# First value weights in idle token and probability buffers, one modulation sum a step and two behind the heads' norm, staging slots refilled later

## What is computed

```
for i in (0, 1):
    ml = silu(c) @ mod_w[i] + mod_b[i]              # 12 column blocks of 512: sh1 sc1 g1 sh2 sc2 g2
    hl = xl * (1 + sc1) + sh1                       # the context: the same with silu(c_ctx)
    i == 0: q, k, v = heads(hl @ wqkv); rope; p = softmax(q k) twice a head
            a = p[0] - lam * p[1];  o = a @ v;  o = o * rsqrt(mean(o^2) + eps) * subln
            yl = o @ wo
    i == 1: yl = pool_mixer(hl)
    xl = layer_norm(ALPHA * xl + (1 + g1) * yl)
    xl = layer_norm(ALPHA * xl + (1 + g2) * experts(xl * (1 + sc2) + sh2))
```

## Time and profile before

| | |
|---|---|
| median of 3 runs | 1258.74 us (1258.15 to 1260.99) |
| the profiled execution | 1261.48 us, of which 1259.6 us are the span from the first to the last instruction |
| busy over the span | TensorE 91%, VectorE 28%, ScalarE 13%, DMA mean 381 GB/s |
| first scores, last scores of the attention | 118.33 us, 253.18 us |
| first expert matmul of layer 0 | 325.45 us |
| granted TensorE clock, mean | 0.972 |

### The profile page before, as it was taken

One profiled execution on the slowest core, in us unless ns is written; L12 is line 12 of the kernel. 1 busy time (PEld: TensorE's weight loads), 2 busy tenths in 40 slices (PEclk: granted clock), 3 DMA queues, 4 the chain that ended last, 5 costly groups with the idle time before them and its releaser, 6 DMA issues.

```text
span 1259.6 us, 12321 instructions
## 1 busy us (share of the span) xinstructions
PE 1141.3 (91%) x5288; PEld 509.4 (40%) x5288; DVE 357.7 (28%) x729; ACT 165.1 (13%) x398; POOL 16.0 (1%) x28
## 2 busy tenths in 40 slices
PE   8969978678899999999999989899999999999995
PEld 3534544444534333343333335634333333433331
DVE  1567889734211111111111113311111111111113
ACT  1101212333200000010000002400000000100000
POOL 0000000000000000000000001000000000000000
PEclk9989988789999999999999999999999999999999
DMA  9898775955599999999999999799999999999993
GB/s 396 336 337 340 281 297 209 422 203 200 213 429 427 427 428 427 428 428 426 429 426 428 428 420 427 311 428 429 426 429 427 428 427 427 429 427 429 427 427 164
DMA packets 37129, 480.17 MB, mean 381 GB/s; under 512 B 4688, under 2 KB 5968, under 8 KB 8016
## 3 DMA queue, kind: packets, MB, share of 16 engines
q1 hardware_dynamic: 33136, 434.96, 82.0%
q0 software_dynamic: 2880, 41.94, 8.8%
q10 hardware_dynamic: 1056, 2.43, 0.6%
HBM read 476.18 MB, written 1.05 MB: 379 GB/s over the span
## 4 chain that ended last, share of the span: by engine, by line
PE 72%; DVE 12%; DMA 11%; issue 2%; ACT 2%; ACTq 0%; DVEq 0%
PE ps L849 51%; DMA ring<-in_mod_w 5%; PE ps L841 5%; PE ps L857 5%; DMA ring<-in_moe_wd 3%; PE ps L710 2%; DVE ring L1258 2%; DVE work L1572 2%; PE ps L613 2%; DVE work L1576 1%; DMA ring<-ring 1%; PE ps L865 1%; DVE modp L1258 1%; PE ps L554 1%; DMA ring<-in_attn_wqkv 1%
## 5 line engine op out<-in xcount | busy, mean ns | idle before, releaser
L849 PE MATMUL ps<-ring,tra 128*64 128x512 f32 x2048 | 446.7, 594 | 1.9 <-ACT tra L1136 1.1
L849 PEld LDWEIGHTS ps<-ring,tra 128*64 128x64 f32 x2048 | 146.0, 137 | 298.3 <-issue 294.8
L849 PE MATMUL ps<-ring,work 128*64 128x512 f32 x1024 | 228.7, 598 | 29.2 <-DVE work L1572 29.2
L849 PEld LDWEIGHTS ps<-ring,work 128*64 128x64 f32 x1024 | 83.1, 137 | 154.1 <-issue 117.3
L1567 DVE TENSOR_TENSOR work<-ps,work 128x512 f32<-128x512 f32 x32 | 22.1, 692 | 279.4 <-ACT work L1143 279.4
L1143 ACT ACTIVATE work<-ps 128x512 f32<-128x512 f32 x32 | 19.1, 597 | 536.7 <-PE ps L849 536.7
L857 PE MATMUL ps<-work,extra 64*128 64x512 f32 x256 | 65.3, 629 | 21.0 <-DVE work L1576 21.0
L1136 ACT ACTIVATE tra<-ps,cols 128x128 f32<-128x128 f32 x128 | 48.2, 456 | 243.8 <-PE ps L841 243.8
L1570 DVE TENSOR_TENSOR work<-work,ps 128x512 f32<-128x512 f32 x32 | 22.0, 689 | 180.7 <-PE ps L849 180.7
L841 PEld LDWEIGHTS ps<-extra,xn 128*128 128x128 f32 x512 | 62.3, 199 | 25.7 <-issue 22.7
L841 PE MATMUL ps<-extra,xn 128*128 128x128 f32 x512 | 68.0, 289 | 2.7 <-DVE extra L1480 2.7
(11 more groups left out here) (182 smaller groups left out, 727.1 us busy)
## 6 DMA issues: line engine op xcount, KB each, us to landing
ring<-in_moe_wg SPq DMA_DIRECT2D x64, 2048.0 KB, 23.1
ring<-in_moe_wu SPq DMA_DIRECT2D x64, 2048.0 KB, 22.8
ring<-in_moe_wd SPq DMA_DIRECT2D x64, 2048.0 KB, 22.1
ring<-in_mod_w POOLq DMA_DIRECT2D x20, 2048.0 KB, 10.6
ring<-in_attn_wqkv SPq DMA_DIRECT2D x5, 2048.0 KB, 15.3
ring<-in_mod_w SPq DMA_DIRECT2D x4, 2048.0 KB, 18.4
ring<-in_attn_wo SPq DMA_DIRECT2D x2, 2048.0 KB, 10.8
ring<-in_tokens SPq DMA_DIRECT2D x2, 1024.0 KB, 16.2
```

Of the source, the lines that this page charges most:

```text
L849: last = mm(ps[SLOTS * h:SLOTS * h + SLOTS, b, :], lhs(k0 + k), w[:, k, h * NB:(h + 1) * NB], start=(k0 + k == 0), stop=(k0 + k == KT - 1) ...
```

## The change

The first value weights (`("v", 0)`) are loaded into `xn` and `tra`, in two halves, with no wait for a slot; they were loaded into slot 0 after k0 had been used. The later attention weights swap slots accordingly: k1 now waits for k0 to be used (it was q0), q1 for q0 (it was v0), v1 for k1, wo0 for q1 as before, wo1 for v1. On VectorE rope batch 0 stands ahead of sum 6 and rope batch 1 behind sum 7, where they stood ahead of sums 4 and 6. Steps 0 to 9 take one whole sum each (sums 8 to 17); sums 18 and 19 are taken behind `norm_heads(1)`. Row batch 3 goes from step 8 to step 9, row batch 4 from step 12 to behind `project(0, 1)`, and the layer-1 `rows_sum` from step 14 into the attention's layer norm. The gate jobs `g1` move from steps 14 and 15 behind the last step, into bank 2 and into `tra`; `gt_0` moves to step 12. The staging slots 2 and 3 are filled with expert units 6 and 7 (they were 2 and 3), whose loads wait for sums 18 and 19; units 2 to 5 take slots 5, 9, 6 and 7.

```diff
-FREE = (4, 8, 2, 3, 5, 9, 6, 7, 0, 1)
+FREE = (4, 8, 5, 9, 6, 7, 2, 3, 1, 0)
...
-         ("q", 0): (1, 2), ("v", 0): (0, 2), ("k", 1): (1, 3), ("q", 1): (0, 3), ("v", 1): (1, 4), ("wo", 0): (0, 4),
-         ("wo", 1): (1, 5)}
-FREED_BY = {("q", 0): ("mod", 1), ("v", 0): ("k", 0), ("k", 1): ("q", 0), ("q", 1): ("v", 0), ("v", 1): ("k", 1),
-            ("wo", 0): ("q", 1), ("wo", 1): ("v", 1)}
+         ("q", 0): (1, 2), ("v", 0): (None, 1), ("k", 1): (0, 2), ("q", 1): (1, 3), ("v", 1): (0, 3), ("wo", 0): (1, 4),
+         ("wo", 1): (0, 4)}
+FREED_BY = {("q", 0): ("mod", 1), ("k", 1): ("k", 0), ("q", 1): ("q", 0), ("v", 1): ("k", 1), ("wo", 0): ("q", 1),
+            ("wo", 1): ("v", 1)}
...
-BATCH_AT = {6: 0, 10: 1, 15: 2, 18: 3, 22: 4}
+BATCH_AT = {6: 0, 10: 1, 15: 2, 19: 3}
...
-HALVES = (2, 3, 2, 3, 2, 2, 3, 2, 3, 2)
+STEP_SUMS = 10
...
-JOB_AT = {10: (0,), 11: (1,), 14: (2,), 15: (3, 4)}
-JOB_BANK = (6, 6, 6, 6, 7, 7, 7, 7, 7, 7, 7)
+JOB_AT = {10: (0,), 11: (1,), 12: (2,)}
+JOB_BANK = (6, 6, 6, 2, 2, 7, 7, 7, 7, 7, 7)
+HEAD_BANK = ((6, 3), (4, 5))
...
+                if unit == ("v", 0):
+                    for half, buf in enumerate((xn, tra)):
+                        load(buf[:, :], attn_wqkv[4][:, half * 2048:half * 2048 + 2048], sem("values_loaded"))
+                    return
...
                 elif v in (2, 3):
-                    sp.wait_ge(sem("summed"), NSUM - 3 + v)
-                elif v in (4, 5):
                     sp.wait_ge(sem("scores_done"), NS)
-                elif v == 6:
+                elif v == 4:
                     sp.wait_ge(sem("pv_done"), NS)
-                elif v == 7:
+                elif v == 5:
                     sp.wait_ge(sem("oT_done"), 2 * TT)
+                elif v in (6, 7):
+                    sp.wait_ge(sem("summed"), NSUM - 7 + v)
...
                 if t == 0:
+                    pe.wait_ge(sem("job_out"), 3)
...
+                if (t, h) == (1, 0):
                     pe.wait_ge(sem("job_out"), EARLY_JOBS)
...
+                    job(3)
                     turn_heads(0)
                     project(0, 0)
+                    job(4)
...
             project(0, 1)
+            row_batch(4)
...
             for n in range(EARLY_SUMS):
-                if n in (4, 6):
-                    rope_batch(n // 2 - 2)
-                for half in range(2):
-                    half_sum(2 * n + half)
+                if n == 6:
+                    rope_batch(0)
+                unit_sum(n)
+            rope_batch(1)
...
-                for i in range(sum(HALVES[:s]), sum(HALVES[:s + 1])):
-                    half_sum(2 * EARLY_SUMS + i)
+                if s < STEP_SUMS:
+                    unit_sum(EARLY_SUMS + s)
...
-                if s == 14:
-                    rows_sum(1)
...
-            for t in range(TT):
-                norm_heads(t)
+            norm_heads(0)
+            job_out(3)
+            norm_heads(1)
+            for n in range(EARLY_SUMS + STEP_SUMS, NSUM):
+                unit_sum(n)
+            job_out(4)
...
+                    if t == 0:
+                        rows_sum(1)
```

More of the change, by code:

```diff
@@ L299, in trunk @@
         ors = small[:, 64:80].rearrange("p (t h) -> p t h", t=TT)
-        ccol, csig = small[:, 0:16], small[:, 16:32]
+        ccol, csig = cols[:, 523:539], small[:, 16:32]
         nT = tra[:, :].rearrange("p (k t) -> p k t", k=KT)
@@ L537, in early_slot @@
             def early_slot(unit):
+                if unit == ("v", 0):
+                    return [buf[:, k * NB:(k + 1) * NB] for buf in (xn, tra) for k in range(4)]
                 return slot(EARLY[unit][0]).rearrange("p (k n) -> p k n", k=KT)
             def early(unit):
+                if unit == ("v", 0):
+                    pe.wait_ge(sem("values_loaded"), 32)
+                    return early_slot(unit)
                 s, n = EARLY[unit]
@@ L614, in multiply @@
                 if kind == "v":
-                    return mm(bank(acc_bank(g)), hT[:, k, t * P:t * P + P], w[:, k, :], start=first, stop=end)
+                    rhs = w[k] if j == 0 else w[:, k, :]
+                    return mm(bank(acc_bank(g)), hT[:, k, t * P:t * P + P], rhs, start=first, stop=end)
                 for n in range(2):
@@ L1261, in half_sum, with unit_sum @@
                             .then_inc(sem("summed"), 1)
+            def unit_sum(n):
+                for half in range(2):
+                    half_sum(2 * n + half)
             def rows_sum(layer):
```

31 lines of the change are left out of this document (14 added, 17 removed).

## The result

The changed kernel took **1250.21 us** (median of 5 runs, 1245.87 to 1251.67); the kernel before, on the same chip, took 1260.99 us (5 runs, 1258.15 to 1263.89). The ratio is 0.9909, with a 95% interval of 0.9894 to 0.9925. It is faster, as forecast, but by about 11 us where 22 were forecast, and it ends 0.2 us outside the range of 1226 to 1250. That margin says nothing by itself: the median of the kernel before was 1258.74 us in the three runs that the forecast started from and 1260.99 us in these five. What counts is that half the gain is missing. The profiled execution took 1251.67 us, its span is 1249.8 us.

What follows compares the result with a forecast made beforehand. The start of the expert matmuls sets the end; ahead of it VectorE's sums need more than TensorE's 9.4 us a step. 1.4 + 18.4 + 3.8 - 1.6 = 22.0 us of gain, forecast 1237 us, 80% range 1226 to 1250.

Steps and rivals of the forecast that it cites:

- first-scores term: Start to the maximum of step 0: 118.2 instead of 119.57 us, a gain of 1.4 us out of 11.5.
- its own lower bound of 5: Up to the first scores: a loss of 5 us if every load there is as slow as the 16 us one.
- The value weights' wait: TensorE's 9.76 us wait ahead of the first value matmuls goes; they start at 70 us.
- rival 1: Staging stays the bound, loads 13 to 16 us throughout, steps to 10 take 105 to 112 us; 1245 to 1256 us; chance 0.17.
- The ten steps: Maximum of step 0 to that of step 10: 97 us instead of 115.4, a gain of 18.4 us.
- Steps 10 to 15 and the turn: From step 10 to the heads' second turn: gains of 3 us and 0.8 us, together 3.8 us.
- Behind the turn: From the turn to the first expert matmul: a loss of 1.6 us, the two moved sums covered with 2 us to spare.
- The refill: Refilling the ring ahead of the experts costs nothing, with some 15 us to spare.
- the third: The term for steps 10 to 15 and the turn: a gain of 3.8 us.
- Rival 2: Loads are quick and the first scores gain 9 to 11 us instead of 1.4; 1227 to 1229 us; chance 0.12.
- The bound of TensorE by itself: By TensorE alone the first scores would start about 9.8 + 2 us earlier, near 106.6 us.
- Rivals 3 and 4: Third: every staging load takes 16 us, 1263 us, chance 0.05. Fourth: refill misses the experts, 1257 to 1260 us, chance 0.03.

Runs made afterwards that it cites:

- Experiment 1: Changed kernel with the q1 load waiting until the first value weights have been used; 1242.74 us, ratio 0.9860 to the kernel before.
- experiments 6: Changed kernel with q1 waiting for the first value weights, k1 for sum 4, and rope batches back ahead of sums 4 and 6; 1239.39 us, ratio 0.9825.
- experiment 12: Changed kernel with the k1 and q1 loads held back, rope batches left where the change puts them; 1242.99 us, ratio 0.9854.
- experiment 2: Changed kernel with the first value weights back in slot 0 and the later attention weights in their old slots and waits; 1241.15 us, ratio 0.9850.
- experiments 6 and 7: The second of the two: changed kernel with value weights back in slot 0 and rope batches back ahead of sums 4 and 6; 1242.50 us, ratio 0.9856.
- Experiment 4: Changed kernel with twelve sums in steps 0 to 9 again and none behind the heads' norm; 1262.65 us, ratio 1.0019.
- experiment 9: Changed kernel with the old refill order, expert units 2 and 3 in staging slots 2 and 3; 1248.65 us, ratio 0.9906.
- experiment 10: Changed kernel with 11 filler products on TensorE ahead of its wait for sum 7 at row batch 1; 1253.60 us, ratio 0.9954.

## Why the prediction was half right

**The step that failed is the first-scores term**, "I laid the loads out: first sum at 48.4 instead of 45.86 (half of the 4.9 us), sums 1 to 5 each bound by a load (9 us alone, 11 to 14 us with one or two others in flight) with sum 5 done at 97". It gave a gain of 1.4 us; the trace gives a loss of 6.9 (maximum of step 0 at 126.50 instead of 119.57), outside its own lower bound of 5. Sum 5 was done at 105.3 us, not 97. The first sum came 1.3 us earlier than laid out. Sums 4 and 5 came late, because the text names k1 and q1 "beside the next ones" but prices the load that meets both at 14 us at most, and 19.4 and 23.8 were measured; two of my own rows spoke against it. The 16 us load of the earlier trace rows was already above the bracket, and the window of 75 to 80 us in the earlier trace rows was full at 328 GB/s, so a unit cost 6.4 us there and not 4.9. Experiment 1 shows it with one load: q1 held back, first scores at the 116 us of the forecast, 7 us off the time. Holding k1 back as well added nothing (experiments 6 and 12).

The forecast also took k1 and q1 as an addition to the old traffic, and they are a replacement: v0 and k1 stood there before, and the staging loads took 16.5 and 18.2 us beside them. That this pair is worse than that one is in the traces (19.3 and 23.8 us). What the traces show beside it is that the small loads behind v0, which I had nowhere in the sum, no longer stand ahead of the second weight load, and that sums 0 to 3 run 2 us later. How much each of them costs stays open.

The cost of it is more than the wait. TensorE stood 12.32 us and did the first scores and part of the next group at the lower level. That part the forecast had, with a shorter wait.

**The value weights' wait** went as forecast, with no bracket ahead of the first value matmuls. They start at 72.76 us, 2.8 us later than the 70 that I gave: TensorE's query group ahead of them starts as much later. But "k1 and q1 are loaded earlier too" stands in that paragraph without a price, and under rival 1 "k1, q1 out of the way" counts as a point for the steps. That was a price to set. As the change stands the edit loses 7 to 9 us (experiment 2, which also puts q1 and the small loads back); with k1 and q1 held back it gains about 3 (experiments 6 and 7).

**The ten steps**: 96.8 us measured, 97 forecast. The two waits for staging loads that I had allowed 4.5 us were one of 3.94 us, ahead of the sum at 168.61 us:

```profile
168.61 0.49 DVE L1269 TENSOR_SCALAR ring<-ring,cols 128x512 f32<-128x512 f32 x1 [3.94 <-DMA ring<-in_mod_w]
```

That row is from VectorE's timeline of the changed kernel. Experiment 4 undoes this part alone and the stretch is 111.0 us.

**Steps 10 to 15 and the turn**: 2.1 us of gain instead of 3, and 1.2 us of loss instead of 0.8 us of gain, together 0.9 instead of 3.8. The second is not settled: the stretch to the turn was 12.4 or 13.6 us in kernels that are alike in it, and 12.4 in the kernel before.

**Behind the turn**: 2.2 us of cost up to the first expert, 1.6 forecast. This too moves: the stretch is 58.2 to 61.1 us in the profiles of the other kernels, 59.8 in this one and 57.6 before. The two moved sums are covered as forecast: the row at 259.27 us above is the first of them, and VectorE waits 3.34 us for TensorE behind them, where I had 2 us to spare. **The refill** costs nothing (experiment 9).

In sum: -6.9 + 18.6 + 0.9 - 2.2 - 0.5 (the experts) = 9.9 us against 22.0. Of the 12.1 us missing, 8.3 are the first term and 2.9 the third.

**Rivals.** Rival 1's time, 1245 to 1256, is where the result lies, but not by its mechanism: it wanted 105 to 112 us in the steps. Its first scores were to come at most 3 us later; they came 6 us later. What it says of loads at 13 to 16 us throughout is refuted: the median load landed after 9.6 us, only three of the twenty sums waited over 3 us for theirs (at 89.02, 99.37 and 168.61 us), and the first two of those loads were slower than it says. Rival 2's 1227 to 1229 wanted all loads quick, and even with k1 and q1 out of the way nobody got the first scores below 114 us. The bound of TensorE by itself, near 106.6 us, was never near. Rivals 3 and 4 did not occur; with the loads as in rival 3 (19 and 24 us, over its 15) it would have needed the steps to be slow too.

## What to carry to other kernels

An earlier transfer frees a place, and the transfers that were waiting for that place move up with it. So do those that stand behind it in program order. List both, and look at what they meet and what was there before, before pricing the one that was moved. Price a load in a stretch by that stretch's own rate at full share (307 to 346 GB/s here), not by the rate of another phase (427), and with all the loads in flight. When an engine is the bound over a chain of steps, taking work out to where it has a wait, as the two sums behind the norm, was worth the whole gain; a weight load that removed a visible 9.8 us wait was worth about 3, by one comparison.

## What the runs showed of the hardware

A staging load took 9.2 us with little beside it and 19.4 and 23.8 us when issued 3.6 us and 9.5 us behind the first of two weight loads on the other queue, while the DMA share stood at 1 and the rate at only 307 to 346 GB/s. I had not expected the rate to be so far under 427 GB/s at a full share. The small packets of the rope swaps fit as the reason. In experiment 12, at the same full share, the rate was 306 GB/s from 70 to 80 us, with the swap copies in flight, and 434 and 429 GB/s from 90 to 110 us, with none and with k1 and q1 on the other queue. No run took the copies away.

A queue's share of the DMA engines followed the size of its packets: three queues with 97, 95 and 95 packets in 5 us had 85.1, 16.1 and 4.3% of the engines' time. In the kernel before, k1 stood behind five small loads on its queue and took 31.4 us, while the staging load on the other queue had most of the time; in the changed kernel k1 and q1 had none ahead of them and took 15.6 and 22.4 us.

The granted clock fell again soon after a filler. In experiment 10 TensorE worked without a break to 117.6 us, waited 1.34 us, worked 1.06 at the full clock, waited 2.46 us for the rope batch, and then ran at a lower clock; in experiment 1 the same 2.46 us wait left the first scores at 1.15 us, and the clock fell only while the next group ran. The windows (columns as in the earlier trace rows) of experiment 10, and below it of experiment 1:

```profile
118.00:120.00 2.00, 1.01 (x8) 0.16 (x8) 1.97 (x4) 0.00 (x0) 0.53 (x1) 1.00 1.01 434
120.00:124.00 4.00, 1.53 (x8) 0.51 (x4) 2.65 (x5) 0.00 (x0) 0.00 (x0) 0.81 0.93 320
124.00:128.00 4.00, 4.00 (x9) 1.71 (x8) 3.18 (x5) 1.45 (x4) 0.00 (x0) 0.76 0.50 213
```

```profile
112.00:116.00 4.00, 1.06 (x8) 0.16 (x8) 3.97 (x4) 0.65 (x2) 0.53 (x1) 1.00 1.00 430
116.00:120.00 4.00, 3.81 (x8) 1.48 (x9) 2.84 (x7) 1.08 (x3) 0.00 (x0) 0.65 1.00 430
```

A mean of 0.65 to 0.81 is a stretch that is partly at the lower level of 1.2 GHz. In experiment 1 the fall landed on the busy work behind the wait. In experiment 10 filling one of two neighbouring waits was not enough.
